# Retention input projections: 16 of 24 weight-row pairs as seven block products ahead of the recurrence

## Chip, core and metric

The kernel runs on one core of a Trainium2 chip. Its engines are TensorE (PE; its weight loads are shown apart as PEld), VectorE (DVE), ScalarE (ACT), GpSimd (POOL) and SyncE (SP), which issues most DMAs. The metric is device time of one launch in microseconds, median of the runs.

## What is computed

One inference step of a two-layer decoder trunk over 1024 prompt tokens and 8 sample tokens, which share all weights and stand side by side as 1032 columns. Layer 0 is sliding-window attention and a gated convolution FFN. Layer 1 is retention and the same FFN. D_MODEL is 1024, retention has 4 heads of key size 256 and value size 512. The part that matters, cut:

```python
def retention_mixer(x, s0, pos, chunk, w_in, w_o):
    hcat = x @ w_in                       # q, k: 4 x 256 each; v, g: 4 x 512 each
    q = retention_rotate(q, pos)          # even, odd columns with cos, sin
    k = retention_rotate(k, pos) * (RET_KEY_DIM ** -0.5)
    o, s_new = retention_chunkwise(q, k, v, s0, chunk)    # scan over 8 chunks of 128
    o = (o - mu) * lax.rsqrt(var + GN_EPS)                # over each head's 512 values
    return (jax.nn.silu(g) * o) @ w_o, s_new

def step(s, inp):                         # one chunk, one head
    inner = jnp.einsum('bihd,bjhd->bhij', qi, ki) * decay_in
    o = jnp.einsum('bhij,bjhe->bihe', inner, vi) + jnp.einsum('bihd,bhde->bihe', qi, s) * q_decay
    s = s * chunk_decay + jnp.einsum('bjhd,bjhe->bhde', ki * k_decay, vi)
```

## The kernel before

**Precision and jobs.** Activations lie transposed, features on partitions and tokens in the free dimension. Each fp32 operand is split into a high and a low part (`wh`, `wl` for weights, `xh`, `xl` for activations), and each product is three matmuls: high by high, high by low, low by high. Every engine has its own program, written out by hand in order, and waits on semaphores. A global list of jobs (`job_order`) numbers the matmul groups of TensorE; the semaphore `jobs` counts them. `bank_table` gives each job its PSUM bank and the job whose result must have left it.

**Weights.** They come as slabs of 128 x 1024 fp32 (512 KB) through three raw buffers (`RAW`, `slabs_to` on SyncE). ScalarE writes the high part (`split_hi`, L1269), VectorE the low part (`split_lo`, L1828); a few low parts are GpSimd's (`lo_table`). `unit_table` and `due_table` say which slot a part goes to and after which job; due times never decrease, so the parts are made in order. `split_upto(job)` makes all that are due by a job.

**The FFN's block products.** In the FFN, pairs of weight rows (t from 2 to 21) are already computed as seven products of half-size blocks (`product`, L952 to 972): the 1032 tokens are cut in two halves (`TH`, 516), each product runs over 4 k-tiles, for two quarters of 258 columns (`TQ`). `weight_sums` on GpSimd makes the weights' four sums in the raw buffer, `xt_raw`, `xt_hi`, `xt_lo` the activations' differences, `copied` (ACT) and `combine` (DVE) bring the results together in `f_ab` and `f_g`. There convolution, Silu and gate of the pair before run at the same time.

**Retention input.** Each head has 12 weight rows of 128: 0 and 1 the even and odd columns of q, 2 and 3 of k, 4 to 7 v, 8 to 11 the gate g. A job `("p", h, j, ch)` is row j for one of three column chunks of 344: 24 matmuls. `plain_out` copies v or applies Silu to g, `rotate` (DVE, four products) and its GpSimd part turn q and k; ScalarE writes them to `scratch_qkvg`. `ret_batch` computes the 36 jobs of head 0 while the last LayerNorm chunks are finished. The jobs of heads 1 to 3 are fillers in the recurrence.

**The recurrence.** 32 periods (`period(i)`, head i div 8, chunk i mod 8). `FILL[i]` holds five lists of jobs. TensorE's order in a period is: `turn` (L1146, L1148, transposes of k and v), fill 0, `inner` (L1154, waits for the split keys `r_kdl`), `back(i-1)` (L1163), first half of `update`, fill 1, second half of `update`, fill 2, `output` (waits for inner and state), fill 3, `sample_out(i-1)` (L1201), fill 4. Heads 1 to 3 put 108 projection jobs in periods 0 to 23 (4 or 5 each); periods 24 to 31 hold 72 output-projection jobs `("o", h, q)` of 12 matmuls, nine each. VectorE's order is `rows` (r_vl L2392, r_kdl L2394), in the second period of a head `masks` and `sample_norm`, then fill 0, `decayed` (L2399), `gated` (L2409), `update`, `inner_lo`, fill 1, `update`, splits, `outer(i-1)` (L2427), fill 2, `norm` (L2443 to 2447), fill 3, `norm_rest` (L2452 to 2458, needs ScalarE's root, L1706), fill 4, splits. ScalarE: `values_hi` (L1660, L1661), `inner_hi`, `gated_hi`, `decay` (L1690), splits, outputs' DMA issues, `queries_hi` (L1666), `state_hi` (L1725), `heads_root`, fill 3 (p_plain L1615, DMA L1617), splits. GpSimd makes the low parts of queries, state and gated values. SyncE loads, in each period, slabs, gates, next queries and values, the next sample state and values. Each period also loads and writes one sample's state of 512 KB; the load waits for the write of two periods ago in the same buffer.

Of the kernel before, what the change touches and what calls it, by code (L numbers as in the profile page):

```python
# [12 lines left out]
P = 128  # L13
# [32 lines left out]
PAIRS_UP = FT - BATCH  # L46
H_PIECES = BATCH * NCH + PAIRS_UP
# [25 lines left out]
def pair_order(t):  # L73

    if t == BATCH:
        return [(sub, n) for n in range(2, 7) for sub in range(2)]
    if t == FT - 1:
        return [(sub, n) for sub in range(2) for n in (0, 1, 2, 3, 5)] + [(sub, n) for n in (4, 6) for sub in range(2)]
    return [(sub, n) for sub in range(2) for n in range(7)]


def up_jobs(L):
# [6 lines left out]
    return out + [("sp", L, t, sub, n) for t in range(BATCH, FT) for sub, n in pair_order(t)]  # L89
# [13 lines left out]
def ret_jobs(h):  # L103

    if h == 0:
        return [(j, ch) for ch in range(NCH) for j in range(5)] + [(j, ch) for j in range(5, NT) for ch in range(NCH)]
    n = NT - 2 if h == RH - 1 else NT
    return ([(2 * p + e, ch) for p in range(2) for ch in range(NCH) for e in range(2)]
            + [(j, ch) for j in range(4, n) for ch in range(NCH)] + [(j, ch) for ch in range(NCH) for j in range(n, NT)])


def job_order():
# [9 lines left out]
    for h in range(RH):  # L122
        jobs += [("p", h, j, ch) for j, ch in ret_jobs(h)]
# [12 lines left out]
def unit_table():  # L136
# [12 lines left out]
    def ffn(L, n, slots, early, start):  # L149
        u0 = len(units)  # L150
        for i in range(2 * BATCH):
            whole(n + i, slots[i], J["up", L, i // 2, i % 2, NCH - 1])
        for p in range(PAIRS_UP):
            for i in range(7):
# [3 lines left out]
                              J["sp", L, BATCH + p, 1, PRODUCT_OF_UNIT[i]]))  # L158
        slot = (start + 7 * PAIRS_UP) // 2
# [13 lines left out]
    for h in range(RH):  # L173
        for j in range(NT):
            whole(n + j, (4, 5, 3, 0, 1, 2)[j % 6] if h == 0 else j % 4, max(J["p", h, j, ch] for ch in range(NCH)))
        n += NT
# [34 lines left out]
def lo_table():  # L211

    mine = set(range(5, 27)) | {U_R + j for j in range(2, 6)} | {U_F1 + j for j in range(2, 7)}
# [12 lines left out]
def pair_index(L, t):  # L226

    return L * PAIRS_UP + t - BATCH


def pair_unit(L, t, i):

    return (U_F0 if L == 0 else U_F1) + 2 * BATCH + 7 * (t - BATCH) + i


def sums_before(n):

# [12 lines left out]
def pair_piece(t):  # L250
# [9 lines left out]
    "copied1": ("T", "pt_in", NB * NG), "hd_hi": ("T", "s_sc", NG), "hd_lo": ("T", "s_tr", NG),  # L260
# [177 lines left out]
def build(nc, A):  # L438
    ctx = ExitStack()
    with ctx:  # L440
# [69 lines left out]
        K.zl = sb("zl", [P, 4, SLAB], F32R)  # L510
        K.g, K.hs0 = [], []
# [143 lines left out]
def x_sum_place(K, n):  # L655
# [3 lines left out]
            (K.xh[:, 0:4, TH:TOK], K.xl[:, 0:4, TH:TOK], K.xr[:, :, TH:TOK]))[n]  # L659

# [2540 lines left out]
```

## Time and profile before

| | us |
|---|---|
| median of 3 runs | 2746.16 (2745.92 to 2748.1) |
| span of the profiled execution | 2744.9 |
| TensorE busy | 2692.8 (98%) |
| VectorE, ScalarE, GpSimd busy | 1638.9, 1036.3, 673.5 |
| layer 0 up to its last FFN job | 0 to 1105 |
| head 0's projections | 1105 to 1241 |
| recurrence, 32 periods | 1241 to 1969 |
| last output projections, FFN of layer 1 | 1969 to 2745 |

Busy time of TensorE is the union of overlapping matmuls, whose modelled durations are longer than the spacing of their starts, so spacing is read from counts over a stretch without idle time. Numbers in brackets behind an instruction are the idle time of its engine just before it and what ended it.

### The profile page before, as it was taken

To read this page: it belongs to the slowest core of one execution; us is meant where nothing else is said; L and a number is where in the kernel's file an instruction comes from. 1 tells how busy PE (TensorE), PEld (TensorE's weight loads), DVE (VectorE), ACT (ScalarE), POOL (GpSimd) and SP (SyncE) were. 2 spreads that over 40 slices of the span, in tenths; PEclk is the share of its full clock that TensorE was granted. 3 is DMA by queue.
4 is the path that set the end of the run, shared out by engine and by line. 5 is a ranking of instruction groups with operands and counts; after the bars stand their busy time and mean duration, and the time that the engine had idled before them with its cause. 6 is when DMAs were issued, how large, how long until landed. Compare 5 with 4: busy or idle time off the path is not lost.

```text
span 2744.9 us, 47495 instructions
## 1 busy us (share of the span) xinstructions
PE 2692.8 (98%) x19166; PEld 2587.3 (94%) x19166; DVE 1638.9 (60%) x3042; ACT 1036.3 (38%) x1930; POOL 673.5 (25%) x534
## 2 busy tenths in 40 slices
PE   8999989999999999999999999999999999999997
PEld 7888879999999999999999999999999999999997
DVE  6556578676767445615446354366688666766455
ACT  5445455433343112323343433432254344332123
POOL 2344351322220002403213122111241223220021
PEclk9999999999999999999999999999999999999999
DMA  4210111222224232235666565686512222223321
GB/s 141 82 44 15 40 33 55 70 86 78 86 78 154 74 112 68 79 111 166 184 197 189 184 194 186 204 267 215 171 55 73 79 84 71 86 96 123 114 73 62
DMA packets 218665, 307.27 MB, mean 112 GB/s; under 512 B 30608, under 2 KB 171536, under 8 KB 218416
## 3 DMA queue, kind: packets, MB, share of 16 engines
q1 hardware_dynamic: 153552, 242.73, 28.0%
q10 hardware_dynamic: 64896, 61.50, 6.6%
q8 instruction: 153, 2.51, 0.4%
q14 instruction: 64, 0.52, 0.1%
HBM read 214.81 MB, written 91.45 MB: 112 GB/s over the span
## 4 chain that ended last, share of the span: by engine, by line
PE 91%; DVE 4%; ACT 2%; issue 1%; POOL 1%; DMA 0%; ACTq 0%; SPq 0%; POOLq 0%; DVEq 0%
PE bank L677 19%; PE bank L679 19%; PE bank L678 18%; PE bank L970 9%; PE bank L972 9%; PE bank L971 9%; PE bank L831 1%; PE bank L810 1%; PE bank L1201 1%; PE bank L1154 1%; PE bank L1163 1%; PE bank L821 1%; PE bank L785 0%; PE bank L1148 0%; DVE y L1866 0%
## 5 line engine op out<-in xcount | busy, mean ns | idle before, releaser
L1828 DVE TENSOR_TENSOR wl<-raw,wh 128x512 fp32r<-128x512 f32 (+1 forms) x381 | 367.6, 971 | 362.8 <-ACT wh L1269 358.4
L677 PE MATMUL bank<-xh,wh 128*128 128x344 f32 x1616 | 525.5, 325 | 1.5 <-DVE f_cv L2135 1.5
L679 PE MATMUL bank<-xh,wl 128*128 128x344 f32 x1616 | 516.8, 320 | 0.0
L678 PE MATMUL bank<-xl,wh 128*128 128x344 f32 x1616 | 516.0, 319 | 0.0
L1269 ACT ACTIVATE wh<-raw 128x512 fp32r<-128x512 f32 (+1 forms) x412 | 307.8, 764 | 367.0 <-PE bank L679 231.0
L970 PE MATMUL bank<-xh,wh 128*128 128x258 f32 x1280 | 362.0, 283 | 0.0
L972 PE MATMUL bank<-xh,wl 128*128 128x258 f32 x1280 | 361.6, 282 | 0.0
L971 PE MATMUL bank<-xl,wh 128*128 128x258 f32 x1280 | 361.1, 282 | 0.0
L1856 DVE TENSOR_TENSOR y<-bank,y 128x344 f32<-128x344 f32 x384 | 192.1, 512 | 231.5 <-PE bank L679 230.7
L677 PEld LDWEIGHTS bank<-xh,wh 128*128 128x128 f32 x1616 | 304.1, 188 | 16.1 <-issue 9.1
L678 PEld LDWEIGHTS bank<-xl,wh 128*128 128x128 f32 x1616 | 303.8, 188 | 4.7
L679 PEld LDWEIGHTS bank<-xh,wl 128*128 128x128 f32 x1616 | 304.0, 188 | 0.0
L971 PEld LDWEIGHTS bank<-xl,wh 128*128 128x128 f32 x1280 | 242.0, 189 | 0.0
L970 PEld LDWEIGHTS bank<-xh,wh 128*128 128x128 f32 x1280 | 241.6, 189 | 0.0
L972 PEld LDWEIGHTS bank<-xh,wl 128*128 128x128 f32 x1280 | 241.4, 189 | 0.0
L2684 POOL TENSOR_TENSOR raw<-raw 128x512 f32<-128x512 f32 x40 | 51.5, 1288 | 589.0 <-DVE wl L1828 588.9
L970 PE MATMUL bank<-x_t2h,wh 128*128 128x258 f32 x640 | 181.0, 283 | 2.0 <-ACT f_ab L1487 2.0
L971 PE MATMUL bank<-x_t2l,wh 128*128 128x258 f32 x640 | 180.9, 283 | 0.0
L972 PE MATMUL bank<-x_t2h,wl 128*128 128x258 f32 x640 | 180.5, 282 | 0.0
L677 PE MATMUL bank<-h_ah,wh 128*128 128x344 f32 x480 | 154.4, 322 | 0.0
L679 PE MATMUL bank<-h_ah,wl 128*128 128x344 f32 x480 | 153.9, 321 | 0.0
L678 PE MATMUL bank<-h_al,wh 128*128 128x344 f32 x480 | 153.3, 319 | 0.0
(294 smaller groups left out, 6202.5 us busy)
## 6 DMA issues: line engine op xcount, KB each, us to landing
raw<-in_w SPq DMA_DIRECT2D x216, 512.0 KB, 3.8
scratch_h<-f_g SPq DMA_DIRECT2D x40, 516.0 KB, 2.7
h_in<-scratch_h SPq DMA_DIRECT2D x30, 688.0 KB, 5.1
scratch_qkvg<-p_plain ACTq DMA_DIRECT2D x96, 172.0 KB, 2.9
r_s<-in_state_in SPq DMA_DIRECT2D x32, 512.0 KB, 3.8
out_state_s<-r_s ACTq DMA_DIRECT2D x32, 512.0 KB, 5.1
scratch_qkvg<-p_rot ACTq DMA_DIRECT2D x24, 344.0 KB, 2.9
xh<-scratch_heads_hi SPq DMA_DIRECT2D x12, 688.0 KB, 8.1
```

The costliest lines, as they stand in the source:

```text
L677: pe.matmul(out, ah, bh, start=(k == 0), stop=False)
L678: pe.matmul(out, ah, bl, start=False, stop=False)
L679: mm = pe.matmul(out, al, bh, start=False, stop=(k == n - 1))
L810: mm = pe.matmul(out, qs[r, q], keys, start=(n_pass == 0), stop=(n_pass == 2))
L821: mm = pe.transpose(bank[5 + half][:, at:at + HD], K.a_prob[r, b % 2, h, t * W:(t + 1) * W], ident[r, r])
L970: pe.matmul(out, hi[:, kk], bh, start=(k == 0 and not adds), stop=False, skip_group_check=adds)
L971: pe.matmul(out, hi[:, kk], bl, start=False, stop=False, skip_group_check=adds)
L972: mm = pe.matmul(out, lo[:, kk], bh, start=False, stop=(k == 3), skip_group_check=adds)
L1269: act.activation(hi, source, ACT.Copy).then_inc(S["hi_done"], 1)
L1828: dve.tensor_tensor(lo, source, hi.bitcast(F32), ALU.subtract).then_inc(S["lo_done"], 1)
L1856: dve.tensor_tensor(t, bank[b][:, 0:CH], t, ALU.add).then_inc(S["yadd"], 1)
L2684: pool.tensor_tensor(g[:, two], g[:, one], g[:, two], ALU.add).then_inc(S["w_sum"], 1)
```

## The change

Of the 48 weight rows, those 32 of q, k and g of head 0 (rows 0 to 3, 8 to 11) and all of heads 1 and 2 become 16 pairs of block products, `RET_PAIRS`, all ahead of the recurrence. Rows 4 to 7 of head 0 are computed as before while LayerNorm ends. Head 3's 12 rows stay plain jobs: four (rows 4 to 7, first chunk, `LEAD`) come right before the recurrence, the other 32 are fillers.

- The FFN's machinery gets a third use, `RET`. Two buffers `f_ab` and `f_g` take the results. `ret_turn` rotates q and k pairs there: 16 products of 258 columns on VectorE and 8 sums on GpSimd per pair; `ret_silu` applies Silu to gate pairs; SyncE writes whole rows of 516 KB. The activations' differences take the place of half of `xh` and `xl`, which are restored (`back_hi`, `back_lo`) after the last pair.
- Fillers: periods 0 to 15 (`MIXED`) hold two projection jobs each, and TensorE puts half a job (12 matmuls) in each of fills 0 to 3. Periods 16 to 31 hold the 72 output jobs, 4 or 5 each, one in each fill. Other engines' work for a projection job stays in fill 1 and fill 3.
- The order of head 3's rows is 4 to 7, 0 to 3, 8 to 11. Splits are made after fill 1, after fill 3 (periods 0 to 15 too), and in the last 16 periods after fill 2.
- SyncE's head loads for the output jobs move to periods 14 to 16 (head 0), 18 (head 1), 23 and 26 (head 2).
- The prologue of the projections takes the FFN's order: both halves of the first chunk's LayerNorm are waited for, and ScalarE's plain outputs alternate with it.

The core of the diff:

```diff
+BATCH_ROWS = (4, 5, 6, 7)
+RET_PAIRS = [(0, 0), (0, 2), (0, 8), (0, 10)] + [(h, j) for h in (1, 2) for j in range(0, 12, 2)]
+END_T = {0: FT, RET: BATCH + PAIRS_RET, 1: FT}
...
+LAST_ROWS = (4, 5, 6, 7, 0, 1, 2, 3, 8, 9, 10, 11)
+LEAD = 4
+
+
+def last_head_jobs():
+
+    return ([(j, ch) for ch in range(NCH) for j in range(4, 8)] + [(2 * p + e, ch) for p in range(2) for ch in range(NCH) for e in range(2)]
+            + [(j, ch) for j in (8, 9) for ch in range(NCH)] + [(j, ch) for ch in range(NCH) for j in (10, 11)])
...
-    for h in range(RH):
-        jobs += [("p", h, j, ch) for j, ch in ret_jobs(h)]
+    jobs += ret_pair_jobs()
+    jobs += [("p", RH - 1, j, ch) for j, ch in last_head_jobs()]
...
+MIXED = 16
+
+
 def fillers():
 
     out = []
-    for h in range(1, RH):
-        jobs = [("p", h, j, ch) for j, ch in ret_jobs(h)]
-        for n in range(NB):
-            at = 36 * n // NB
-            to = 36 * (n + 1) // NB
-            part = jobs[at:to]
-            out.append([part[0:1], part[1:2], part[2:3], part[3:4], part[4:]])
+    jobs = [("p", RH - 1, j, ch) for j, ch in last_head_jobs()][LEAD:]
+    for n in range(MIXED):
+        a, b = jobs[2 * n:2 * n + 2]
+        out.append([[], [a], [], [b], []])
     jobs = [("o", h, q) for h in range(RH - 1) for q in range(24)]
-    for n in range(NB):
-        part = jobs[9 * n:9 * n + 9]
-        out.append([part[0:2], part[2:4], part[4:6], part[6:7], part[7:9]])
+    for n in range(NI - MIXED):
+        part = jobs[9 * n // 2:9 * (n + 1) // 2]
+        out.append([part[0:1], part[1:2], part[2:3], part[3:4], part[4:]])
...
+    def ret_pairs(u):
+        ret_batch(u)
+        for t in range(BATCH, END_T[RET]):
+            for sub, n in pair_order(RET, t):
+                product(RET, t, sub, n)
+        for j, ch in last_head_jobs()[:LEAD]:
+            for half in range(2):
+                ret_half(("p", RH - 1, j, ch), half)
...
-    def fill(jobs):
-        for key in jobs:
-            if key[0] == "p":
-                ret_project(*key[1:])
-            else:
-                ret_out(key)
+    def fill(i, s):
+
+        if i < MIXED:
+            if s < 4:
+                ret_half(FILL[i][s // 2 * 2 + 1][0], s % 2)
+            return
+        for key in FILL[i][s]:
+            ret_out(key)
...
+    def ret_turn(t, first, last):
...
+            dve.wait_ge(S[f"comb{sub}"], START[f"comb{sub}"] + 4 * pair_index(RET, t) + 4)
+            dve.tensor_tensor(even, b[:, c], sin, ALU.mult).then_inc(S["rt_prod"], 1)
+            dve.tensor_tensor(odd, a[:, c], sin, ALU.mult).then_inc(S["rt_prod"], 1)
+            dve.tensor_tensor(a[:, c], a[:, c], K.cosR[:, c], ALU.mult).then_inc(S["rt_prod"], 1)
+            dve.tensor_tensor(b[:, c], b[:, c], K.cosR[:, c], ALU.mult).then_inc(S["rt_prod"], 1)
...
+    def ret_pairs():
+        weight_sums(RET, BATCH)
+        weight_sums(RET, BATCH + 1)
+        for t in range(BATCH, END_T[RET]):
+            ret_turn(t)
+            if t + 2 < END_T[RET]:
+                weight_sums(RET, t + 2)
...
-        if i == 24:
+        if i == 18:
             heads_written(16, 2)
             for ch in range(NCH):
                 heads_landed(ch, 1)
                 heads(1, ch)
```

## Rows read from the trace of the kernel before

**Rows 1.** The page: busy time of TensorE, and the chain that ended last.
```profile
PE 2692.8 (98%) x19166; PEld 2587.3 (94%) x19166; DVE 1638.9 (60%) x3042; ACT 1036.3 (38%) x1930; POOL 673.5 (25%) x534
...
PE 91%; DVE 4%; ACT 2%; issue 1%; POOL 1%; DMA 0%; ACTq 0%; SPq 0%; POOLq 0%; DVEq 0%
```

**Rows 2.** Stretches: us, busy and count of each engine, clock, DMA share, GB/s.
```profile
540.00:800.00 260.00, 260.00 (x2174) 260.00 (x2173) 176.02 (x286) 103.35 (x206) 71.31 (x52) 1.00 0.23 80
1145.00:1241.00 96.00, 96.00 (x611) 96.00 (x611) 14.63 (x20) 19.39 (x31) 5.41 (x6) 1.00 0.39 125
1241.00:1969.00 728.00, 725.75 (x4637) 682.16 (x4636) 373.44 (x717) 257.63 (x408) 169.36 (x127) 1.00 0.63 197
```

**Rows 3.** Timeline of TensorE, end of the LayerNorm: start us, us, instruction, [idle before].
```profile
1144.82 0.43 PE L710 MATMUL bank<-xh,wh 128*128 128x344 f32 x1 [0.90 <-DVE xl L1893]
```

**Rows 4.** TensorE from the end of output() in period 6 to inner() in period 7.
```profile
1393.07 0.40 PE L679 MATMUL bank<-r_sh,r_qkl 128*128 128x512 f32 x1
...
1397.99 0.60 PE L1148 MATMUL bank<-ident,r_cxv 128*128 128x128 f32 x4
...
1402.19 0.50 PE L1154 MATMUL bank<-r_cxq 128*128 128x128 f32 x3
```

**Rows 5.** ScalarE over the same period boundary.
```profile
1394.95 1.28 ACT L1706 ACT_TABLE_LOAD   x1
1396.24 0.20 ACT L1706 ACTIVATE r_st<-r_st 128x1 f32<-128x1 f32 x1
1396.46 1.28 ACT L1615 ACT_TABLE_LOAD   x1
...
1398.24 0.34 ACTq L1617 DMA_DIRECT2D scratch_qkvg<-p_plain  x1
1398.69 0.60 ACT L1660 ACTIVATE r_vh<-bank 128x512 fp32r<-128x512 f32 x1 [0.47 <-PE bank L1148]
```

**Rows 6.** VectorE over the same period boundary.
```profile
1399.93 0.47 DVE L2394 SCALAR_TENSOR_TENSOR r_kdl<-bank,r_dec,r_kdh 128x256 fp32r<-128x256 f32 x1
```

**Rows 7.** VectorE at the end of period 9: rotation, then the norm's rest.
```profile
1463.20 0.52 DVE L2353 TENSOR_TENSOR p_prod<-bank,cosR 128x344 f32<-128x344 f32 x1 [1.77 <-PE bank L679]
...
1464.90 0.15 DVE L2452 RECIPROCAL r_st<-r_st 128x1 f32<-128x1 f32 x1
...
1465.34 0.81 DVE L2458 TENSOR_SCALAR r_ga<-bank,r_st 128x512 f32<-128x512 f32 x1
```

**Rows 8.** VectorE in period 9: sample_norm() from its first copy to decayed().
```profile
1446.21 0.42 DVE L2464 COPY r_xu<-bank 8x256 f32<-8x256 f32 x1
...
1449.30 0.27 DVE L2399 TENSOR_TENSOR r_inn<-bank,r_dec 128x128 f32<-128x128 f32 x1
```

**Rows 9.** All engines at the start of period 24: two splits ahead of inner().
```profile
1787.19 2.01 ACT L1269 ACTIVATE wh<-raw 128x1024 fp32r<-128x1024 f32 x2 [0.47 <-ACT p_plain L1615]
...
1788.28 2.36 DVE L1828 TENSOR_TENSOR wl<-raw,wh 128x1024 fp32r<-128x1024 f32 x2 [7.01 <-ACT wh L1269]
...
1791.16 0.47 DVE L2394 SCALAR_TENSOR_TENSOR r_kdl<-bank,r_dec,r_kdh 128x256 fp32r<-128x256 f32 x1
...
1791.69 0.49 PE L1154 MATMUL bank<-r_cxq 128*128 128x128 f32 x2 [1.06 <-DVE r_kdl L2394]
```

**Rows 10.** DMA issues by tile: count, KB each, median us from issue to landing.
```profile
scratch_qkvg<-p_plain ACTq DMA_DIRECT2D x96, 172.0 KB, 2.9
...
out_state_s<-r_s ACTq DMA_DIRECT2D x32, 512.0 KB, 5.1
...
xh<-scratch_heads_hi SPq DMA_DIRECT2D x12, 688.0 KB, 8.1
...
r_cxv<-scratch_qkvg SPq DMA_DIRECT2D x32, 256.0 KB, 6.1
```

**Rows 11.** A stretch at the end of attention (columns as in rows 2) and its stall.
```profile
379.00:387.00 8.00, 5.61 (x21) 5.64 (x22) 5.99 (x11) 6.71 (x10) 3.75 (x5) 0.57 0.29 101
...
381.39 0.63 PE L677 MATMUL bank<-a_oh,wh 128*128 128x344 f32 x1 [2.74 <-DVE a_ol L2013]
```

More of the change, by code:

```diff
@@ L147, in unit_table, with pair_units @@
         n += 5
[L149 to L153, printed above, removed]
+    def pair_units(L, n, early, start):
+        for p in range(END_T[L] - BATCH):
             for i in range(7):
@@ L158, in ffn @@
                               J["sp", L, BATCH + p, 1, PRODUCT_OF_UNIT[i]]))
+    def ffn(L, n, slots, early, start):
+        u0 = len(units)
+        for i in range(2 * BATCH):
+            whole(n + i, slots[i], J["up", L, i // 2, i % 2, NCH - 1])
+        pair_units(L, n, early, start)
         slot = (start + 7 * PAIRS_UP) // 2
@@ L172, in unit_table @@
     u_r, s_r = len(units), n
[L173 to L176, printed above, removed]
+    for i, j in enumerate(BATCH_ROWS):
+        whole(n + i, (4, 5, 2, 3)[i], J["p", 0, j, NCH - 1])
+    pair_units(RET, n, 0, 0)
+    n += 2 * END_T[RET]
+    for i, j in enumerate(LAST_ROWS):
+        whole(n + i, (0, 2, 3, 1)[i % 4], J["p", RH - 1, j, NCH - 1])
+    n += NT
     s_o = n
@@ L211, in lo_table @@
 def lo_table():
[L213 removed]
+    mine = set(range(5, 27)) | {U_R + j for j in range(2, 7)} | {U_F1 + j for j in range(2, 7)}
     on_pool, nth, seen = [], [], [0, 0]
@@ new lines, in ret_batch, with halves, whole @@
+    def ret_batch(u):
+        def halves(tiles, ch, half):
+            for t, kind in tiles:
+                key = ("p", 0, BATCH_ROWS[2 * t + kind], ch)
+                if ch == 0 and half == 0:
+                    wait_slab(pe, S, ret_slab(0, key[2]))
+                up_half(key, ret_slab(0, key[2]), ch, half)
+        def whole(t, kind, ch):
+            halves([(t, kind)], ch, 0)
+            halves([(t, kind)], ch, 1)
+        pe.wait_ge(S["n_lo"], 2 * u + 2)
+        var(u + 1)
+        whole(0, 0, 0)
+        whole(0, 1, 0)
+        mean(u + 2)
+        whole(1, 0, 0)
+        whole(1, 1, 0)
+        for n in range(2):
+            product(RET, BATCH, 0, n)
+        for ch in (1, 2):
+            tiles = batch_tiles(ch)
+            pe.wait_ge(S["n_lo"], 2 * (u + ch) + 1)
+            halves(tiles[:2], ch, 0)
+            if ch == 1:
+                var(u + 2)
+            pe.wait_ge(S["n_lo"], 2 * (u + ch) + 2)
+            halves(tiles[:2], ch, 1)
+            for t, kind in tiles[2:]:
+                whole(t, kind, ch)
+        for n in range(2):
+            product(RET, BATCH, 1, n)
@@ L1627, in project, with ret_silu, plain @@
             plain_out(h, j, ch)
+    def ret_silu(t):
+        if RET_PAIRS[t - BATCH][1] < 8:
+            return
+        m = 4 * pair_index(RET, t)
+        for tile, count in ((K.ab[:, t % 2, 2:2 + TOK], 2), (K.g[t % 2][:, :], 4)):
+            for sub in range(2):
+                act.wait_ge(S[f"comb{sub}"], START[f"comb{sub}"] + m + count)
+            act.activation(tile, tile, ACT.Silu).then_inc(S["rt_silu"], 1)
     def ret_batch(u):
-        jobs = ret_jobs(0)
+        def plain(t, kind, ch):
+            plain_out(0, BATCH_ROWS[2 * t + kind], ch)
@@ L1632, in ret_batch @@
         split_next(2)
         root(u + 1)
-        split_next(1)
-        normal(u + 1, 0)
-        normal(u + 1, 1)
-        split_next(1)
-        squares(u + 2)
-        for j, ch in jobs[0:5]:
-            project(0, j, ch)
+        split_next(2)
+        plain(0, 0, 0)
+        normal(u + 1, 0)
+        plain(0, 1, 0)
+        plain(1, 0, 0)
+        squares(u + 2)
+        normal(u + 1, 1)
+        plain(1, 1, 0)
+        split_next(1)
         root(u + 2)
+        plain(0, 0, 1)
+        plain(1, 0, 1)
@@ L2180, in xt_raw @@
         out = x_sum_place(K, n)[2]
+        if n == 0 and L == RET:
+            dve.wait_ge(S["jobs"], J["fin", 0, 23])
         if n == 0 and L == 1:
@@ L2967, in period @@
                 heads(1, ch)
-        if i == 27:
+        if i == 23:
+            heads_written(16 + 3, 2)
+            sp.wait_ge(S["jobs"], J["o", 0, 23])
+            heads_landed(0, 2)
+            heads(2, 0)
+        if i == 26:
             heads_written(24, 3)
-            sp.wait_ge(S["jobs"], J["o", 0, 23])
-            for ch in range(NCH):
+            for ch in (1, 2):
                 heads_landed(ch, 2)
```

409 lines of the change are left out of this document (295 added, 114 removed).

## The prediction

> **What bounds the kernel now.** I read the page first: TensorE is busy for 98% of the span and carries 91% of the chain that ended last, so the question is how many matmul slots go and how many stalls come [rows 1]. Then the stages [rows 2]. A busy share says little here; the spacing of matmul starts says more. In the block products of layer 0 (540 to 800 us) there are 2174 matmuls of 258 columns in 260.00 us with no idle time: 119.6 ns each. In the projections of head 0 (1145 to 1241 us) there are 611 matmuls of 344 columns in 96.00 us: 157.1 ns each. The recurrence (1241 to 1969 us) is as dense, 725.75 busy of 728 us, although VectorE, ScalarE and GpSimd each work there in a chain that is many short steps long. What keeps TensorE full is the filler: 108 projection jobs of 24 matmuls (3.77 us each) and 72 output jobs of 12 (1.89), 543 us in all, 17.0 of a period's 22.7. 5.8 us of its own work are left to each of the 32 periods. Over projections and recurrence TensorE stalls only four times: 0.90 us for the normalized third column chunk, and 1.02, 0.16 and 1.06 us for the low part of the decayed keys (r_kdl) ahead of inner() (the first [rows 3], the last [rows 9]).
>
> **Step 1: the products.** A pair of weight rows costs 2 x 3 x 24 = 144 matmuls of 344 columns, 144 x 0.1571 = 22.62 us. As 7 products on 2 column quarters each it costs 7 x 2 x 12 = 168 of 258 columns, 168 x 0.1196 = 20.09 us. 16 pairs save 16 x 2.53 = 40.5 us, all on TensorE's path. The same machinery runs stall-free in layer 0 [rows 2]; here VectorE's rotation (16 products per rotated pair, 6 pairs) takes the place of convolution and gate, and GpSimd's 8 sums come before the weight sums, which wait for their own slabs anyway. VectorE is at 176.02 of 260 us there, so I book nothing for the steady pairs. The trace of before doesn't show this mix; from below it can't be under 0, from above one stall as at a product stage's entry, about 1 us, in each rotated pair: 0 to 6 us. The entry (input differences, four plain rows) loses the 0.90 us stall and may get one of the same size: +1.
>
> By the Trainium skill (TensorE: Matmul & The Clock Gate, section Back-to-back issue gap) a stream of weight load and matmul takes about 81 ns at 128 columns and 131 ns at 512. A line through the two gives, as an estimate, 109 ns at 344 and 98 ns at 258, so 15.7 us a pair direct and 16.5 us as products: the change would lose 0.8 us a pair. The rows say 157.1 and 119.6 ns and decide.
>
> **Step 2: the recurrence loses its cover.** It does the same own work, but periods 0 to 15 now hold two jobs instead of 4 or 5, each cut in halves of 1.89 us in the slots where whole jobs of 3.77 us lay; periods 16 to 31 hold 4 or 5 jobs of 12 matmuls, one to a slot, also 1.89 us. So every wait that 3.77 us covered is now covered by 1.89. I lay out one period boundary [rows 4 to 6], with E the end of output()'s last matmul (1393.07 + 0.40 = 1393.47). TensorE: turn() of the next period starts at 1397.99, E + 4.52, with one job between; with half a job E + 2.64. From turn() to inner() it is 4.20 us with a job, 2.32 with half: inner() wants to start at E + 4.96. What it waits for: ScalarE copies the turned values 0.70 after turn() starts, VectorE ends r_kdl 1.71 after that copy's start (1398.69 to 1400.40), TensorE starts 0.06 later [rows 5, 6, 9]. That is E + 2.64 + 0.70 + 1.77 = E + 5.11. A period in which nothing else lies there stalls by about 0.1 us: 15 of them, 1.5 us. The others:
> - **Table switches** (the last four rows are gates and take Silu, the norm takes Sqrt; 10, 12, 13, 14): after E ScalarE does r_sh, a table load of 1.28, the root, another load of 1.28, the copy and its DMA, and is free only at 1398.58, E + 5.11 [rows 5]. The value copy then starts at 5.13 instead of 3.34, inner() at 6.90: 1.9 us each, 7.7. Before, the longer job hid just this. Period 11 has a weight split besides, 3.2.
> - **Rotation** (4, 5, 7, 8): rotate() is queued ahead of norm_rest() on VectorE. It starts at the job's end, E + 1.95, takes 1.70 to the reciprocal, then 0.44 + 0.81 to the end of r_ga and 1.05 more to the end of r_kdl [rows 6, 7]: E + 5.95, so 1.0 each, 4.0.
> - **Weight splits**: 1.0 us each on ScalarE and 1.2 on VectorE [rows 9]. Where one falls ahead of outer() and one at the period's end (2, 3, and 6 with a rotation) they delay by 2.1, 2.1 and 2.2. At the end of period 15 three slabs come free at once (their due times are in order) behind two table loads: 5.2. Before, two splits with a whole job of cover stalled 1.06 [rows 9], which agrees with this way of counting.
> - **Samples** (9, 17, 25): sample_norm() holds VectorE from 1446.21 to 1449.30, 3.1 us ahead of decayed() and update() [rows 8]. The second update's bank comes free late by 1.6 (2.1 with an add before it), and in period 9 the norm, two splits and a rotation follow late: 5.0, 2.15, 2.15.
> - **Start and change of head** (0, 8): 0.9 together.
> - **Output fillers** (16 to 31): one split at the end of 19 and 20, 0.9 and 0.6; 1.45 each in 26 and 30, where the split lies ahead of norm_rest(); 0.5 for the heads' starts.
> Sum: 1.5 + 7.7 + 3.2 + 4.0 + 6.4 + 5.2 + 9.3 + 0.9 + 4.9 = 43.1 us. From below, a stall can't be negative, and the four old cases show 3.1 us with more cover; if only table switches, period 15 and the samples count it is 25. From above the delays add where I let them overlap: 60.
>
> By the Trainium skill (ScalarE: Activation LUTs, section What ACT_TABLE_LOAD costs) each switch takes a drain of about 1.38 us beside the 1.28. Here the root starts 0.01 us after the load ends (1394.95 + 1.28 to 1396.24), so the row decides; by the page the 6 gate periods would cost 12 x 1.38 = 16.6 us more, 2767 us.
>
> **Step 3: DMA and the queues.** The recurrence moves the same states, chunks and heads, but a period shrinks from 22.7 to about 15.1 us (441 of work and 43 of stalls by 32). DMA share is 0.63 now, at a mean of 197 GB/s [rows 2], so 14.3 us of engine time and 4.5 MB a period; 76 jobs leave, each with 172 KB out [rows 10] and a third of a 512 KB weight slab in, 0.8 MB a period. By bytes that leaves 11.7 of 15.1 us, an estimated share of 0.77. A state's write lands after 5.1 us in the median, SyncE waits for it ahead of the next state, and r_cxv behind it lands after 6.1 [rows 10]; its slack shrinks by the 7.6 us that the period loses. The six loads of head 1 now come in period 18. I take 3 us; bounds 0, and 30 if the landing binds each second period by 2 us.
>
> **Sum**, against the profiled span of 2744.9 us (the median of the runs is 1.3 us above it): 2744.9 - 40.5 - 3.1 (old stalls) + 1 + 43.1 + 3 = 2748.4, with nothing for the steady pairs, whose nearest row shows none. As a median 2750 us.
>
> **The rivals.**
> - **The cover is enough** (gain stays): engines start early where I lined them up, and stalls come to 20. Then 2727 + 1.3, about 2728. For it: VectorE is busy for only 51% of the stage, ScalarE for 35% [rows 2]. Against: the order is fixed on each, and rows 5 to 7 are chains, not loads.
> - **The DMA chain binds** (slower): state write, SyncE's wait, state and values behind it. It decides once a write takes over some 8 us (an estimate: the 5.1 of now and 3 us of slack), since the next values then land after their turn(). 30 us more: 2780. For: the share of 0.77, and 8.1 us to land for a head load [rows 10]; against: TensorE never waits for a DMA in the stage now.
> - **The clock falls**: around a stall of 2.74 us the granted clock was at 0.57 in the mean from 379 to 387 us, so mostly at 1.2 GHz instead of 2.4 [rows 11]: some 3.4 us lost. If that follows each of the long stalls I forecast (periods 9, 11, 15) as much each, 2760. Against: stalls of 1 us left it at 1.00 throughout the recurrence [rows 2].
> - **The products don't save**: the rotated pairs, with VectorE and GpSimd on the same tiles, hold TensorE by 2 us or more each, and the entry too: 2765.
>
> **How the numbers follow.** Forecast case 0.52 (2735 to 2762 by itself), cover enough 0.23, DMA 0.12, clock 0.08, products 0.05. A measurement of this kernel tells 0.2%, 5.5 us, from no change. Of the forecast case 0.12 lies below 2740.7, 0.21 within, 0.19 above 2751.7; with 0.21 of the first rival faster and the last three slower: faster 0.33, same 0.23, slower 0.44. The range for 8 in 10 reaches from the first rival to the DMA case: 2724 to 2779.
>
> **What would show it.** Starts of block products 119.6 ns apart in 16 pairs of about 20.1 us and hardly a stall in them: step 1. The recurrence taking 728 - 287 (the 76 jobs moved) = 441 us of work plus some 43 of stalls, most of them in front of inner() and ended by r_kdl, the largest at the starts of periods 10 and 16, about 1.9 us after each gate period: step 2. SyncE's wait for the state write and no wait for r_cxv: step 3. Were the stalls ended by DMA instead, or did TensorE wait less than 25 us, or the clock show halves, the prediction is wrong there.

## The result and the profile after

The changed kernel takes 2778.92 us (median of 4 runs, 2777.93 to 2779.73) beside 2746.59 us before (median of 4 runs too): a ratio of 1.0118, with a 95% interval of 1.0106 to 1.013. It is slower by 1.2%. The forecast named slower as the likeliest sign and 2750 us as the time. The time lies 29 us above that and at the very end of the range. The profiled execution has a span of 2776.6 us against 2744.9.

First the page of the changed kernel: its span, busy times and the chain that ended last. These lines answer to [rows 1].

```profile
span 2776.6 us, 48978 instructions
PE 2676.2 (96%) x19550; PEld 2562.7 (92%) x19550; DVE 1777.0 (64%) x3282; ACT 1095.5 (39%) x2085; POOL 763.1 (27%) x611
...
PE 85%; DVE 7%; ACT 3%; issue 2%; DMA 1%; POOL 1%; ACTq 0%; SPq 0%; POOLq 0%; DVEq 0%
```

TensorE has only 16.6 us less to do by busy time, where the products alone should give 40.5. Its share of the chain fell from 91 to 85%, and VectorE's rose from 4 to 7%.

Then the stages, with the columns of [rows 2]: a stretch of the pairs, and the whole recurrence from its first `turn` to its last `back`.

```profile
1160.00:1470.00 310.00, 310.00 (x2591) 310.00 (x2591) 181.38 (x331) 118.54 (x241) 126.37 (x108) 1.00 0.30 104
...
1486.60:2002.90 516.30, 465.00 (x2826) 413.43 (x2824) 326.99 (x645) 196.35 (x322) 144.10 (x103) 0.96 0.73 227
```

The same stretch of the kernel before:

```profile
1241.20:1971.00 729.80, 727.55 (x4649) 683.94 (x4647) 375.06 (x719) 258.70 (x409) 169.36 (x127) 1.00 0.63 197
```

The pairs run without one idle microsecond: 310.00 us for 2591 matmuls of 258 columns, 119.6 ns each. The loss is in the recurrence. By the rows of before it should take 727.55 - 76 x 3.77 = 441.0 us of work. It takes 465.0 us of work and 51.3 of idle time. So there are two losses, 51.3 us in which TensorE waits and 24.0 us more of work. For most of the second the granted clock has the reason: 0.96 in the mean over 516.3 us is 4% or 21 us, where it was 1.00 before. Read in finer windows, the clock falls eleven times to half and costs 22.2 us in all, 19.7 of them while TensorE works and the rest inside its waits. The other 4.3 us aren't the clock's: without its falls the work of every kernel below (in e3 without the repeated matmuls too) comes to 444 to 447 us instead of 441. What these 4 us are is open.

TensorE's waits of the recurrence, by what ended them (us in total, times, longest):

```profile
PE bank L1257 <- DVE r_kdl L2638: 40.5, 22, 5.3
PE bank L1249 <- DMA r_cxq<-scratch_qkvg: 5.8, 1, 5.8
PE bank L743 <- DVE r_state L2661: 4.9, 3, 1.8
```

L1257 is `inner`, L1249 the first transposes of `turn`, L743 with r_state the second `update`. Some of these waits one by one, from TensorE's timeline:

```profile
1492.14 0.58 PE L1257 MATMUL bank<-r_cxq 128*128 128x128 f32 x1 [2.88 <-DVE r_kdl L2638]
...
1535.29 0.49 PE L1257 MATMUL bank<-r_cxq 128*128 128x128 f32 x2 [2.30 <-DVE r_kdl L2638]
...
1568.50 0.38 PE L1257 MATMUL bank<-r_cxq 128*128 128x128 f32 x1 [0.78 <-DVE r_kdl L2638]
...
1644.79 0.38 PE L1257 MATMUL bank<-r_cxq 128*128 128x128 f32 x1 [3.06 <-DVE r_kdl L2638]
...
1680.09 1.22 PE L1257 MATMUL bank<-r_cxq 128*128 128x128 f32 x4 [3.18 <-DVE r_kdl L2638]
...
1747.79 0.58 PE L1257 MATMUL bank<-r_cxq 128*128 128x128 f32 x1 [5.29 <-DVE r_kdl L2638]
...
1765.00 0.66 PE L1249 MATMUL bank<-ident,r_cxq 128*128 128x128 f32 x2 [5.83 <-DMA r_cxq<-scratch_qkvg]
...
1924.61 0.38 PE L1257 MATMUL bank<-r_cxq 128*128 128x128 f32 x1 [2.50 <-DVE r_kdl L2638]
```

The clock around them, in windows of the same trace:

```profile
1531.00:1549.00 18.00, 15.70 (x91) 14.00 (x91) 11.22 (x19) 7.38 (x14) 5.04 (x4) 0.91 0.76 238
1697.00:1740.00 43.00, 38.03 (x239) 33.64 (x240) 21.44 (x45) 21.71 (x34) 11.02 (x8) 1.00 0.75 228
1678.00:1694.00 16.00, 13.91 (x70) 12.47 (x71) 6.82 (x12) 6.13 (x9) 3.21 (x3) 0.79 0.54 180
```

Behind the stall of 2.30 us the clock is at 0.91 in the mean over 18 us. Around the one of 3.18 us it is at 0.79 over 16 us, so at 1.2 GHz for some 7 of them. The first of these falls costs 1.7 us, the second 3.4; nine of the eleven are of the first size. Over the 43 us that hold three stalls of 1.8 to 1.9 us it is at 1.00.

### The profile page after: what moved, and what is told of

Same layout as the page of the kernel before. It is cut to its first block, busy times and chain, and to the rows that moved or that the text cites. A ratio compares the mean times of both kernels' runs of the same rounds, so it can differ in the third digit from the quotient of the medians.

```text
span 2776.6 us, 48978 instructions
## 1 busy us (share of the span) xinstructions
PE 2676.2 (96%) x19550; PEld 2562.7 (92%) x19550; DVE 1777.0 (64%) x3282; ACT 1095.5 (39%) x2085; POOL 763.1 (27%) x611
## 4 chain that ended last, share of the span: by engine, by line
PE 85%; DVE 7%; ACT 3%; issue 2%; DMA 1%; POOL 1%; ACTq 0%; SPq 0%; POOLq 0%; DVEq 0%
PE bank L1036 13%; PE bank L1038 13%; PE bank L1037 13%; PE bank L743 12%; PE bank L745 12%; PE bank L744 12%; PE bank L776 2%; PE bank L778 2%; PE bank L777 2%; DVE wl L2004 1%; PE bank L897 1%; PE bank L876 1%; PE bank L1257 1%; ACT wh L1372 1%; PE bank L1266 1%
## 5 line engine op out<-in xcount | busy, mean ns | idle before, releaser
L1036 PE MATMUL bank<-xh,wh 128*128 128x258 f32 x1792 | 506.2, 283 | 0.0
L1037 PEld LDWEIGHTS bank<-xl,wh 128*128 128x128 f32 x1792 | 338.4, 189 | 0.0
L1036 PEld LDWEIGHTS bank<-xh,wh 128*128 128x128 f32 x1792 | 337.9, 189 | 0.0
L1038 PEld LDWEIGHTS bank<-xh,wl 128*128 128x128 f32 x1792 | 337.6, 188 | 0.0
L1036 PEld LDWEIGHTS bank<-x_t2h,wh 128*128 128x128 f32 x896 | 168.9, 189 | 2.3 <-DVE wl L2004 2.3
L1038 PEld LDWEIGHTS bank<-x_t2h,wl 128*128 128x128 f32 x896 | 169.2, 189 | 0.0
L1037 PEld LDWEIGHTS bank<-x_t2l,wh 128*128 128x128 f32 x896 | 169.2, 189 | 0.0
L743 PE MATMUL bank<-xh,wh 128*128 128x344 f32 x488 | 162.3, 333 | 1.5 <-DVE f_cv L2311 1.5
L776 PE MATMUL bank<-xh,wh 128*128 128x344 f32 x472 | 156.3, 331 | 2.7 <-DVE xl L2069 2.4
L744 PE MATMUL bank<-xl,wh 128*128 128x344 f32 x488 | 157.0, 322 | 0.0
L745 PE MATMUL bank<-xh,wl 128*128 128x344 f32 x488 | 156.9, 322 | 0.0
```

The lines of the kernel that those rows point to most:

```text
L743: pe.matmul(out, ah, bh, start=(k == 0), stop=False)
L744: pe.matmul(out, ah, bl, start=False, stop=False)
L745: mm = pe.matmul(out, al, bh, start=False, stop=(k == n - 1))
L776: pe.matmul(out, ah, xh[:, k, c], start=(k == 0), stop=False)
L1036: pe.matmul(out, hi[:, kk], bh, start=(k == 0 and not adds), stop=False, skip_group_check=adds)
L1037: pe.matmul(out, hi[:, kk], bl, start=False, stop=False, skip_group_check=adds)
```

## The experiments

Three theories stood against each other. **A**: the filler was cut into halves, so what stands in ScalarE's and VectorE's queues ahead of r_kdl shows as stalls, and the long ones halve the clock behind them, which costs as much again as a part of the stalls. **B**: VectorE, ScalarE or the DMA engines have no room in periods of 13 to 19 us, wherever the work stands. **C**: the waits are set by SyncE's order of loads. Each median is of 4 to 10 launches.

All kernels side by side. Idle and busy are TensorE's in the recurrence, from the first `turn` to the last `back`, read from windows as above, in us.

| kernel | median us | ratio to before (95%) | length | busy | idle |
|---|---|---|---|---|---|
| changed | 2778.92 | 1.0118 (1.0106 to 1.013) | 516.3 | 465.0 | 51.3 |
| e1_heads_late | 2769.03 | 1.0084 (1.0069 to 1.0099) | 504.3 | 458.3 | 46.0 |
| e2_no_silu | 2758.81 | 1.0045 (1.003 to 1.006) | 494.4 | 457.3 | 37.1 |
| e3_repeat | 2766.33 | 1.0071 (1.0054 to 1.0088) | 504.9 | 473.3 | 31.6 |
| e4_late | 2773.76 | 1.0094 (1.0073 to 1.0114) | 511.5 | 463.1 | 48.4 |
| e5_slabs_behind | 2747.84 | 1.0007 (0.9998 to 1.0016) | 485.7 | 458.5 | 27.2 |
| e6_all | 2738.92 | 0.9976 (0.9965 to 0.9986) | 471.4 | 449.6 | 21.8 |
| e7_filled | 2739.46 | 0.9973 (0.9964 to 0.9983) | 471.0 | 450.8 | 20.2 |
| e8_whole | 2758.39 | 1.0044 (1.003 to 1.0059) | 495.7 | 456.5 | 39.2 |
| e9_later_whole | 2747.55 | 1.0004 (0.9995 to 1.0014) | 481.4 | 451.9 | 29.5 |
| e10_part | 2733.59 | 0.9954 (0.9941 to 0.9968) | 470.2 | 451.0 | 19.2 |

**e1: the heads' loads.**

```diff
-        if i == 16:                     # ahead of slabs, gates, queries, values
-            sp.wait_ge(S["jobs"], J["p", 3, 11, 2])
-            heads(0, 2)
...
+        if i == 16:                     # end of the period
+            sp.wait_ge(S["jobs"], J["p", 3, 11, 2])
+            heads(0, 2)
```

> Only SyncE's order changes: the two loads of head 0's last column chunk (688 KB each) stand at the end of period 16 instead of at its start, behind the slabs, gates, queries and values of the next period. In the changed kernel TensorE waits 5.8 us at the start of period 17 for r_cxq, with the granted clock at half after it. Theory A (it is the place in the queue): this stall goes, about 7 us with its clock, 2772 against 2779. Rival B (the DMA engines are simply full there, share 0.79 to 1.07 from 1740 to 1765): the wait only moves, at most 2 us gained.

It gained 9.9 us. The stall of 5.83 us at 1765.00 is gone, idle time fell by 5.3 us and busy time by 6.7. So the wait was the place in SyncE's queue. In the changed kernel this queue shows it itself:

```profile
1741.76 0.70 SPq L3242 DMA_DIRECT2D xh<-scratch_heads_hi  x1
1742.50 2.96 SPq L3242 DMA_DIRECT2D xl<-scratch_heads_lo  x1
1745.50 3.37 SPq L3065 DMA_DIRECT2D raw<-in_w  x3
1749.04 0.48 SPq L3215 DMA_DIRECT2D r_cxg<-scratch_qkvg  x1
1749.56 1.68 SPq L3217 DMA_DIRECT2D r_xs<-scratch_qkvg  x1
1751.34 4.73 SPq L3192 DMA_DIRECT2D r_cxq<-scratch_qkvg  x1
```

Two loads of 688 KB and three slabs of 512 KB stand ahead of r_cxq, which took 12.8 us to land instead of 5.9. The gain was larger than the 7 us expected because of the busy time, and that part isn't the edit's by any mechanism shown: at the start of period 0, at the second update of period 25 and at the start of 31 TensorE waits as before (2.81, 1.78 and 2.49 us), but no fall of the clock comes with these waits here, where each had one in the changed kernel.

**e2: without the table loads.** Copy instead of Silu for head 3's gate jobs.

```diff
-... ACT.Copy if j < 8 else ACT.Silu)
+... ACT.Copy if j < 8 or h == RH - 1 else ACT.Silu)
```

> Head 3's twelve gate jobs in periods 10 to 15 are copied without Silu, so ScalarE loads no table between root and copy; this leaves out the Silu of head 3's gates. Theory A (my step 2: table loads and the copy behind them delay the value copy): the stalls at the starts of periods 11 to 16 (1.9, 3.2, 1.8, 1.8, 1.9 and 5.3 us) fall by 1.8 to 2.6 each, 11 to 12 us in all, and with the two or three clock falls that follow them 15 us, 2764. Without relief of the clock 11 us, 2768. Rival B (VectorE's or the DMA's side sets these waits): under 4 us.

It gained 20.1 us, 14.2 of it idle time and 7.7 busy time. The stalls at the starts of periods 11, 13, 14 and 15 (1.91, 1.83, 1.83, 1.90) are gone entirely, that of period 12 fell from 3.18 to 0.34 and that of 16 from 5.29 to 3.83. With the 11.8 us of these six, the gain stands where theory A put it; the rest is a shorter wait at the start (2.88 to 2.16) and at the second update of period 17 (1.80 to 0.38), and the clock, which falls six times instead of eleven.

**e3: work where TensorE idled.** 12 matmuls are done twice in ten periods, ahead of `inner`.

```diff
+            if s == 0 and i in (0, 3, 4, 7, 10, 11, 12, 13, 14, 15):
+                ret_half(FILL[i][1][0], 0, thrown=True)     # start and stop, result overwritten
             if s < 4:
                 ret_half(FILL[i][s // 2 * 2 + 1][0], s % 2)
```

> In ten periods whose inner() waited 1.8 to 3.2 us (0, 3, 4, 7, 10 to 15) TensorE does 12 matmuls of the first filler half twice, once for nothing: 120 matmuls, 18.9 us more work, put where it idled. Output unchanged. Theory A (the granted clock halves after a long idle time, and that costs 24 us over the recurrence besides the stalls): stalls fall by 18.3 us, work rises by 18.9, and the clock falls after the starts of periods 0, 3, 4, 10, 11 and 12 are gone, 10 us: 2769. Rival B (matmuls there are slow for another reason, and filling idle time brings nothing): 2779 to 2780. Rival C (the clock falls anyway a little later): same time as B, with falls at other places.

18.9 us of work more, and the kernel is 12.6 us faster. Idle time fell by 19.7 us and busy time rose by only 8.3 us, so the same matmuls as before took 10.6 us less. Here are 30 us around the place where the changed kernel stalled for 3.18 us and then ran at a clock of 0.79:

```profile
1670.00:1700.00 30.00, 28.70 (x183) 25.66 (x182) 14.15 (x30) 15.60 (x25) 8.43 (x6) 1.00 0.64 199
```

This decides for the clock: nothing on any other engine was changed, and the slow matmuls went with the idle time ahead of them. That run's rival C (the falls come elsewhere) is out in the main: five falls are left of eleven and cost 10.2 us instead of 22.2. One of the five is new, at the second update of period 17, where a wait of 1.78 us (1.80 in the changed kernel, without a fall) stands in both.

**e4: work behind the next value copy.**

```diff
             values_hi(i)                       # ScalarE; on VectorE: rows(i)
+        if 1 <= i <= NI:
+            fill(FILL[i - 1][3])
+            fill(FILL[i - 1][4])
...
+            split_upto(J[(FILL[i - 1][4] or FILL[i - 1][3])[-1]], U_F1)   # behind gated_hi, inner_lo
...
-        fill(FILL[i][3])
...
-        if i < NI:
-            split_upto(J[FILL[i][3][-1]], U_F1)
-        fill(FILL[i][4])
```

> ScalarE's and VectorE's work for the job in fills 3 and 4 (plain output with its Silu, rotation, additions) moves behind the next period's value copies and r_vl, r_kdl, and the weight splits at the period's end move behind inner_lo() and gated_hi(). The work is the same, only its place changes. Theory A (what stands in both queues ahead of the value copy makes nearly all stalls at inner()): of the 40 us at inner() at most 8 stay, with some 15 us of halved clock gone too, so about 45 us less, 2734; the 5.8 us for r_cxq and 5 us at the samples' update stay. Rival B (VectorE and ScalarE have no room in the short periods): stalls move to the second update or to output(), under 15 us gained, 2765 or more. Rival C (DMA binds as soon as the engines don't): stalls turn into waits for r_cxv or r_cxq.

A miss: 5.2 us instead of 45. The four launches lie far apart, from 2763.81 to 2777.28 us, and the trace is of one of the longer ones (2774.75), so the 5.2 is rough. But the waits at `inner` fell as expected, from 40.5 to 10.3 us. What came in their place is in TensorE's waits:

```profile
PE bank L1249 <- DMA r_cxq<-scratch_qkvg: 18.5, 4, 11.1
PE bank L1249 <- issue: 10.8, 3, 4.9
PE bank L1257 <- DVE r_kdl L2638: 10.3, 8, 3.8
PE bank L743 <- DVE r_state L2661: 7.9, 3, 3.8
```

The waits are where rival C put them, though not for its reason, as e5 shows. SyncE's queue shows what holds r_cxq:

```profile
1640.93 0.44 SPq L3237 DMA_DIRECT2D r_vb<-scratch_rows  x1
1649.22 0.33 SPq L3066 DMA_DIRECT2D raw<-in_w  x1
1649.60 0.44 SPq L3216 DMA_DIRECT2D r_cxg<-scratch_qkvg  x1
1650.13 0.45 SPq L3193 DMA_DIRECT2D r_cxq<-scratch_qkvg  x1
1650.63 0.66 SPq L3203 DMA_DIRECT2D r_cxv<-scratch_qkvg  x1
1658.58 0.35 SPq L3230 DMA_DIRECT2D r_s<-in_state_in  x1
```

```profile
1658.98 0.45 PE L1249 MATMUL bank<-ident,r_cxq 128*128 128x128 f32 x1 [4.87 <-issue]
```

SyncE waits 7.9 us (1641.37 to 1649.22) until the late split frees the raw buffer of the next slab. Only then the chunks go out: r_cxq at 1650.13, which lands after 6.7 us, and r_cxv at 1650.63, which takes 8.3 us, to 1658.9. `turn` needs both and has waited 4.87 us then. Waits of this kind are the second largest of SyncE in this kernel's recurrence:

```profile
SPq L3066 <- DVE wl L2004: 123.6, 23, 11.9
```

I had moved the splits and not looked at who waits for them.

**e5: the same, with the slab behind the chunks.**

```diff
-        if i:
-            slabs_to(min(due_by(J[(FILL[i - 1][4] or FILL[i - 1][3])[-1]]), S_F1) + RAW)
         if live:
             gates(i)
             if i + 1 < NI:
                 queries(i + 1)
                 values(i + 1)
+        if i:
+            slabs_to(min(due_by(J[(FILL[i - 1][4] or FILL[i - 1][3])[-1]]), S_F1) + RAW)
```

> As e4_late, and on SyncE the weight slabs freed by the last period stand behind the loads of gates, next queries and next values instead of ahead of them. In e4_late SyncE sat before such a slab until VectorE had made the late split (1640.93 to 1649.22 us), then before a state's write, and the next r_cxq landed late: 29.3 us of stalls at turn(). Theory A (these are order in SyncE's queue, not bandwidth): about 23 of the 29.3 us go and the halved clock behind them, some 12 us, 2739; the 6 us at the start of period 17 stay, since the heads' loads still lie ahead there. Rival B (the DMA engines are full in periods this short): stalls for r_cxq stay above 15 us, 2760 or more.

It gained 25.9 us on e4_late, idle time fell from 48.4 to 27.2. Of the 29.3 us at `turn` (18.5 ended by r_cxq, 10.8 shown as issue) the 6.8 at the start of period 17 stay. It is order and not bandwidth: the DMA share over the recurrence is 0.78 here against 0.73 in e4_late, with fewer waits. The time is that of the kernel before. I expected 2739; busy time fell by only 4.6 us where 12 were expected, as the clock still fell six times, beside waits of 6.8 us for r_cxq, 3.8 at an update, and 3.2, 2.9, 2.2 and 2.0 us.

**e6: everything together.** Also e1's order, and `sample_norm` behind `inner_lo`.

```diff
-        if n == 1 and h:
-            sample_norm(h - 1)         # VectorE, ahead of decayed()
...
             inner_lo(i)
+        if n == 1 and h:
+            sample_norm(h - 1)
...
             update(i, 1)
+        if n == 1 and h:
+            sample_norm_rest(h - 1)
```

> As e5_slabs_behind, with e1_heads_late's order of the heads' loads, and with sample_norm() behind inner_lo() and sample_norm_rest() behind the second update on VectorE (ScalarE's root of the samples behind decay()). Theory A (all the loss is order in four queues): stalls in the recurrence of some 12 us, of halved clock 5, so 458 us from the first turn() to the last back() against 516.3, 2720, below the kernel before. Rival B (a resource binds at some 15 us a period): 2745 or more.

2738.92 us: faster than before (interval 0.9965 to 0.9986), short of the 2720 expected. The waits:

```profile
PE bank L1257 <- DVE r_kdl L2639: 15.8, 12, 3.2
PE bank L1249 <- DMA r_cxq<-scratch_qkvg: 4.1, 2, 3.2
```

The samples' 4.9 us at `update` shrank to 0.7, but `inner` waits in the periods behind them: 2.4 us at the start of 10 (3.06 in the changed kernel) and 3.2 at that of 26, where it was 0.7. In period 25 of the changed kernel VectorE, the third pair of numbers below, is busy for 15.92 of 19.47 us, so it has little room, as B says. But it isn't full, and B isn't shown: in e6 a split of 2.48 us at 1877.15 stands ahead of `norm_rest` and r_kdl there, and e10, which moves this split behind the next `inner_lo` and the samples back, has no wait at the start of 26.

```profile
1885.96:1905.43 19.47, 17.69 (x103) 15.60 (x102) 15.92 (x38) 6.73 (x12) 5.07 (x4) 0.91 0.60 178
```

**e8: whole jobs in fills 0 and 3**, the rest as in the changed kernel.

```diff
-            if s < 4:
-                ret_half(FILL[i][s // 2 * 2 + 1][0], s % 2)
+            if s in (0, 3):
+                for half in range(2):
+                    ret_half(FILL[i][1 if s == 0 else 3][0], half)
```

> The changed kernel with one edit on TensorE: in periods 0 to 15 the two jobs stand whole in fills 0 and 3 (24 matmuls, 3.8 us each) and fills 1 and 2 are empty, instead of a half in each of fills 0 to 3. Theory A (the halves are too short in front of inner(), where before whole jobs lay): the 32.8 us of stalls at inner() up to period 16 shrink to about 3; new stalls of 0.9 us appear in front of each second update, which now waits for VectorE's first (0.75 us and a semaphore), 14 us; all below the length after which the clock fell, so 17 us of halved time go too: 2749. Rival B (the order of the fillers doesn't matter, only their total): 2775 or more.

It gained 20.5 us of the 30 expected. The new wait is there, of the expected size, in each of the first 16 periods (0.87 to 0.93 us; 2.40 in period 9):

```profile
1654.86 0.47 PE L743 MATMUL bank<-r_vh,r_kdh 128*128 128x512 f32 x1 [0.93 <-DVE r_state L2662]
```

At `inner` 6.3 us of wait stay up to the start of period 16 instead of 32.8, where 3 were expected: 3.83 of them at the start of 16, behind the three splits. The total of the filler is the same in both kernels, so its place matters: a whole job in front of `inner` covers what a half doesn't.

**e7 and e9: two more placements.** e7 is e6 with head 0's loads another period later, six output jobs in periods 17 and 25, and two plain outputs behind the first value copy. e9 is e7 with e8's whole jobs.

```diff
-        part = jobs[9 * n // 2:9 * (n + 1) // 2]
+        at = [0, 4, 10, 14, 18, 22, 27, 31, 35, 39, 45, 49, 54, 58, 63, 67, 72]
+        part = jobs[at[n]:at[n + 1]]
```

> As e6_all, with the loads of head 0's second and third column chunk for the output jobs in periods 16 and 17, behind the values of the next period; with six output jobs instead of five in periods 17 and 25 (four instead of five in 19 and 23); and with the plain outputs of the last two jobs ahead of the recurrence behind the first value copy. Theory A (each large stall left in e6_all has its own place): the stall at the start of period 0 falls from 2.9 to under 1 us, those for r_cxq at the starts of periods 16 and 17 (0.9 and 3.2) go, those at inner() of periods 18 and 26 fall by up to 1.9: stalls 21.8 to 13, 2729. Rival B (work per period binds, the stalls move to the next period): 2737 or more.

> e7_filled and e8_whole together. Theory A: in e7_filled the wait at inner() is down to 0.2 us in a plain period, so whole jobs there buy nothing and the empty fills 1 and 2 cost 0.9 us in each of 16 periods: 10 to 14 us slower than e7_filled. Rival B (the late work of e7_filled needs longer cover at inner()): faster than e7_filled.

e7 stands where e6 stands, 10 us short of the 2729 expected. The waits at the starts of periods 0, 16 and 17 for which it was made are gone (2.9, 0.9 and 3.2 us). Two new ones came, 2.2 and 2.65 us, the second of them this:

```profile
1862.99 0.43 PE L744 MATMUL bank<-xh,wh 128*128 128x344 f32 x1 [2.65 <-DVE y L2037]
```

The matmuls that wait are the next period's first output job. The jobs use three banks in turn, so with six in period 25 it needs the bank of that period's fourth, and the addition that empties it stands behind the next r_kdl now. e9 is 8.1 us slower than e7, a little under the 10 to 14 of theory A: when the waits at `inner` are short already, whole jobs only bring 13.0 us of waits at the second update.

**e10: the placements that paid.**

```diff
+        if 1 <= i <= MIXED:
+            fill(FILL[i - 1][3])       # late up to period 15 only
...
+        if i >= MIXED:
+            fill(FILL[i][3])           # in its old place from 16 on
```

> What e4 to e7 gained, without what they lost: in periods 0 to 15 the last job's evacuation stands behind the next value copies as in e7_filled; from period 16 on the additions stand where the changed kernel has them, and samples of heads 1 to 3 too (those of head 0 behind inner_lo()); all end-of-period and mid-period splits stand behind the next inner_lo(); loads of head 0 as in e7_filled; output jobs 4 or 5 a period as in the change. Theory A: in the first 16 periods the 7 us of stalls of e7_filled; after them the two waits for additions (4.9 us) go, the stalls of 0.9, 0.9, 2.5 and 2.5 us behind splits go, 3.6 us at the samples' updates come back: 12 us of stalls instead of 20.2, and 2.5 us less behind the recurrence: 2727. Rival B (each stall taken away comes back one period later, since VectorE is at 14 to 17 us in periods of 16 to 19): 2736 or more.

2733.59 us, 0.46% faster than before (0.9941 to 0.9968) and 1.6% faster than the change as given, the fastest of the kernels here. 7 us were missing from what I expected, and as much in idle time, 19.2 instead of 12 (the trace is of the slowest of the five launches, 2737.17 us). The largest part is new: `sample_out` waits for `outer` (r_s):

```profile
PE bank L1304 <- DVE r_s L2674: 8.2, 3, 3.3
PE bank L1257 <- DVE r_kdl L2641: 8.1, 9, 2.3
PE bank L743 <- DVE r_state L2664: 4.3, 3, 1.8
```

In two of the three cases VectorE isn't busy ahead of `outer`, it waits for a load of SyncE. Here is the largest:

```profile
1877.47 3.68 SPq L3248 DMA_DIRECT2D xl<-scratch_heads_lo  x1
1884.40 0.34 SPq L3235 DMA_DIRECT2D r_s<-in_state_in  x1
1884.80 0.44 SPq L3242 DMA_DIRECT2D r_vb<-scratch_rows  x1
...
1892.94 1.41 DVE L2674 SCALAR_TENSOR_TENSOR r_s<-r_vb,r_k,r_s 128x512 f32<-128x512 f32 x2 [5.54 <-DMA r_vb<-scratch_rows]
...
1894.50 0.40 PE L1304 MATMUL bank<-r_s,r_qm 128*8 128x256 f32 x4 [3.32 <-DVE r_s L2674]
```

The sample's state and values go out only at 1884.40 and 1884.80, behind loads of heads and a wait of 3.2 us for a state's write, and land some 8 us later. The case at 1771.24 is of the same kind (VectorE waits 6.16 us for r_vb). Only in the third, at 1966.58, `outer` stands right behind two late splits. No run moved these loads, so what they cost is read and not tested.

## Why the prediction was right and wrong, step by step

**Step 1, the products: right.** 119.6 ns was booked and measured, no stall in a rotated pair. From the first matmuls of head 0's projections to the first `turn` the changed kernel has 1486.6 - 1241.2 = 245.4 us more, where 286.5 - 40.5 - 0.9 + 1.0 = 246.1 was the sum. The entry has one stall of 1.00 us, as booked:

```profile
1101.15 0.53 PE L797 MATMUL bank<-n_sq,ones 128*128 128x344 f32 x1 [1.00 <-issue]
```

**Step 2, the stalls: right in place, nearly so in size.** 43.1 us were the sum, 45.5 came besides the wait for r_cxq. Term by term, forecast and measured: table switches 1.9 each, measured 1.91, 1.83, 1.83 and 1.90; period 11 3.2, measured 3.18; rotations 1.0, measured 0.78; splits 2.1, 2.1, 2.2, measured 2.30, 2.29, 2.12; end of period 15 5.2, measured 5.29; samples 5.0 in period 9 and 2.15 in 17 and 25, measured 4.42, 1.80 and 2.46. Two terms were too small: start and change of head with 0.9, where the first two `inner` wait 2.88 and 1.10 us, and the splits of periods 26 and 30 with 1.45 each, which give 2.50 and 2.49. The plain periods had 1.5 and gave nothing. So the total is closer than its terms: what is missing in some is made up by others. That these waits are the queue's order is shown by e2 (the table loads), e4 (40.5 to 10.3 us at `inner`) and e8 (whole jobs).

For the start the reason was not in my layout: the two buffers of p_plain were waited for, one DMA landing per output (in e6_all ScalarE sits 5.62 us for it). e7 put two of the four outputs behind the value copy and the stall went.

**Step 2, the table load.** The drain of 1.38 us beside the 1.28 of a load, which the Trainium skill gives (ScalarE: Activation LUTs, section What ACT_TABLE_LOAD costs), is not in the stalls: with it the gate periods would wait 1.9 + 2 x 1.38 = 4.7 us, an estimate, and they wait 1.83 to 1.91. The trace disagrees with it here. Of matmul spacing the estimate by a line through the two figures of the Trainium skill (TensorE: Matmul & The Clock Gate, section Back-to-back issue gap) gave 98 ns at 258 columns; the pairs ran at 119.6.

**Step 3, DMA: size nearly right, cause only half.** 3 us were booked, one stall of 5.83 us came. The booked mechanism, the state's write holding the chunks, shows in no stall by itself in the changed kernel: SyncE waits 252.7 us in all for those writes against 271.3 before (a larger share of a shorter recurrence), and their landing fell from 5.1 to 3.5 us in the median. The DMA share came out at 0.73 where 0.77 was estimated. The stall came from the move of the head loads, which I had listed in the change for head 0 and priced for head 1 alone. This was a DMA moved in SyncE's queue without what stands behind it being named.

**The clock: the step that failed.** It was a rival with a chance of 0.08 and 3 x 3.4 = 10 us. The work grew by 24.0 us, 19.7 of them by the clock and 4.3 for a reason not known; with these the span's forecast of 2748.4 gives 2772.4, with the 5.2 us more of idle time 2777.6; the span is 2776.6. The sum itself had the clock's falls at nothing. The rival had three at 3.4 us each, and eleven came: nine cost 1.7 us and two 3.4. So the count was far too small and the price of most falls twice too large. The count went wrong because I let a fall follow only the three stalls above 3 us, although my one row of a fall had a stall of 2.74 us and the row against had none above 1.06 [rows 11, 2]. Nine stalls of my own layout, of 1.9 to 2.2 us, lay in between with no row for either side, and I put them all on the side of no fall. In the trace eleven stalls are of 1.8 to 2.5 us; six went with a fall and five didn't, and all five longer ones went with one. The bound from above should have taken them in. The 2780 of the DMA rival is near the measured time by chance; its mechanism isn't in the trace.

**The range** held the time only because its end was that rival's.

## What to carry to other kernels

A filler that is removed is not worth its matmul time but that minus the waits that it hid, and each wait must be laid out from the chain of every engine behind the last matmul; that layout came out here within 3 us of 43. Idle time that lets the clock fall is paid for beyond its length (here 1.7 us more for most falls), so put a price on that, or put any work there: 18.9 us of useless matmuls made the kernel 12.6 us faster. And when work is moved back in one queue, look first at what waits for it in the others: the same edit was worth 5 us with SyncE's slabs ahead of the chunks and 31 with them behind. Lastly, a total that agrees doesn't show its terms, and a clock's falls differ from kernel to kernel at waits that are the same, so a difference of a few us needs the trace and not only the time.

## What the runs showed of the hardware

The same stall doesn't always bring the fall of the clock. In the changed kernel the 2.30 us at 1535.29 were followed by it (0.91 over 18 us), and three of 1.8 to 1.9 us weren't, while the one of 1.91 us at 1661.81 was. In e2_no_silu a stall of 2.29 us at the same place wasn't followed by one. In e6_all one of 3.19 us wasn't followed, and one of 2.08 us was, the latter with the next 7 us at 0.76:

```profile
1747.10 0.41 PE L1249 MATMUL bank<-ident,r_cxq 128*128 128x128 f32 x2 [3.19 <-DMA r_cxq<-scratch_qkvg]
...
1744.00:1760.00 16.00, 12.79 (x77) 11.85 (x77) 9.27 (x21) 5.99 (x11) 5.28 (x5) 1.00 1.03 323
1943.00:1950.00 7.00, 6.88 (x33) 6.46 (x34) 4.81 (x10) 3.05 (x4) 1.29 (x1) 0.76 0.47 162
```

In the traces here a fall costs 1.7 us, or twice that, and once four times (beside the wait of 11.1 us in e4). The length of the stall alone doesn't decide between 1.8 and 3.2 us whether one comes; what else does stays open. In no traced recurrence a fall came without a stall of at least 1.8 us beside it.
